# Kernel matmuls directly behind the chunk inputs, late pieces between them, and routing of two token tiles ahead of the third

## What is computed

```python
mod = silu(cond) @ w_ada + b_ada            # 1024 x 6144: shift, scale, gate, twice
h = rms_norm(x) * (1 + sc1) + sh1
u = h @ ssm_w_in
# per 16-channel group, both directions: complex diagonal recurrence of 64 states
h_t = a * h_(t-1) + B u_t;  y = u * D + Re(C h) of both directions
m = gelu(y) @ w_glu;  x = x + g1 * (val * sigmoid(gate))
h2 = rms_norm(x) * (1 + sc2) + sh2
scores = sigmoid(h2 @ router_w); biased = scores + router_b
# best of 4 groups by the sum of its two largest, then the two best experts in it;
# weights = their scores over their sum
y = sum over the chosen e of weight_e * ((silu(h2 @ w_gate[e]) * (h2 @ w_up[e])) @ w_down[e])
x = x + g2 * y;  out = rms_norm(x)
```

## Time and profile before

| | us |
|---|---|
| Median of 3 runs | 860.6 (858.01 to 864.39) |
| The profiled execution | 861.62 |
| Its span in the trace | 859.3 |
| PE busy | 741.9 (86%) |
| DVE busy | 301.7 (35%) |
| ACT busy | 184.9 (22%) |

### The profile page before, as it was taken

How to read it: one execution, slowest core, us unless ns; L and a number is a source line. 1 busy time by engine, 2 the same in 40 slices (tenths; PEclk the granted TensorE clock), 3 DMA queues, 4 the chain that set the end, 5 groups by cost and what they waited for, 6 DMA issues and landing times.

```text
span 859.3 us, 22717 instructions
## 1 busy us (share of the span) xinstructions
PE 741.9 (86%) x9653; PEld 410.0 (48%) x9654; DVE 301.7 (35%) x861; ACT 184.9 (22%) x389; POOL 56.1 (7%) x98
## 2 busy tenths in 40 slices
PE   5799777487989985999997999999999999999830
PEld 5345453176554455545552644554554555455320
DVE  3788769998004235112211111201201212111017
ACT  3554241111022231022211021201201202221113
POOL 1000000530010001100000000000000000000000
PEclk9889897756999985999999999999999999999975
DMA  8900439770108680899999999999999999999933
GB/s 340 412 18 2 167 130 400 281 252 6 51 19 282 208 333 1 314 409 409 411 410 411 409 410 411 409 411 410 410 410 380 412 410 411 410 410 410 411 112 152
DMA packets 70010, 259.15 MB, mean 302 GB/s; under 512 B 10728, under 2 KB 10776, under 8 KB 65864
## 3 DMA queue, kind: packets, MB, share of 16 engines
q1 hardware_dynamic: 66968, 254.02, 75.3%
q0 software_dynamic: 1632, 3.20, 1.0%
q10 hardware_dynamic: 1360, 1.19, 0.6%
HBM read 252.49 MB, written 6.29 MB: 301 GB/s over the span
## 4 chain that ended last, share of the span: by engine, by line
issue 56%; PE 23%; DVE 9%; DMA 3%; POOL 3%; ACT 2%; POOLq 2%; ACTq 1%; SPq 0%; DVEq 0%
PE ps L1035 6%; PE ps L1095 3%; PE ps L984 2%; PE ps L887 2%; PE ps L970 1%; PE ps L927 1%; POOL y_scratch L501 1%; DVE sreg L1336 1%; PE ps L819 1%; PE ps L792 1%; ACTq L665 1%; DVE vreg L1336 1%; POOLq L519 1%; PE ps L992 1%; PE ps L946 1%
## 5 line engine op out<-in xcount | busy, mean ns | idle before, releaser
L1129 PE MATMUL ps<-ring,vreg 128*32 128x512 f32 x2240 | 245.7, 593 | 14.3 <-DMA ring<-in_moe_w_up 9.6
L1129 PEld LDWEIGHTS ps<-ring,vreg 128*32 128x32 f32 x2240 | 72.2, 110 | 180.6 <-issue 160.3
L1136 PE MATMUL ps<-ring,vreg 128*32 128x256 f32 x2240 | 124.2, 380 | 0.0
L1121 PEld LDWEIGHTS ps<-vreg,sreg 128*128 128x128 f32 x816 | 96.1, 196 | 15.1 <-issue 13.4
L1121 PE MATMUL ps<-vreg,sreg 128*128 128x96 f32 x816 | 99.8, 280 | 1.5 <-DVE vreg L1567 1.5
L1597 DVE TENSOR_TENSOR vreg<-vreg,ps 128x256 f32<-128x256 f32 x48 | 17.3, 415 | 223.5 <-ACT vreg L743 223.5
L1136 PEld LDWEIGHTS ps<-ring,vreg 128*32 128x32 f32 x2240 | 71.2, 110 | 46.8
L1608 DVE COPY vreg<-ps 32x256 f32<-32x256 f32 x96 | 40.7, 424 | 105.8 <-PE ps L1136 103.3
L755 ACT ACTIVATE vreg<-ps 32x256 f32<-32x256 f32 x96 | 35.8, 373 | 148.1 <-PE ps L1136 146.1
L743 ACT ACTIVATE vreg<-ps 128x256 f32<-128x256 f32 x48 | 15.0, 384 | 210.0 <-PE ps L1129 210.0
L1035 PE MATMUL ps<-ring 128*128 128x512 f32 x128 | 56.1, 595 | 1.4 <-issue 0.7
(11 more groups left out here) (268 smaller groups left out, 590.2 us busy)
## 6 DMA issues: line engine op xcount, KB each, us to landing
ring<-in_moe_w_gate SPq DMA_DIRECT2D x128, 512.0 KB, 12.9
ring<-in_moe_w_up SPq DMA_DIRECT2D x128, 512.0 KB, 14.4
ring<-in_moe_w_down SPq DMA_DIRECT2D x128, 512.0 KB, 12.7
ring<-in_w_ada SPq DMA_DIRECT2D x24, 1024.0 KB, 11.0
ring<-in_ssm_w_glu SPq DMA_DIRECT2D x8, 1024.0 KB, 11.9
ring<-in_ssm_w_in SPq DMA_DIRECT2D x8, 512.0 KB, 21.8
ring<-y_scratch SPq DMA_DIRECT2D x6, 512.0 KB, 6.3
tmat<-ada_rows SPq DMA_DIRECT2D x4, 512.0 KB, 5.4
```

The source lines that it names most:

```text
L1121: last = pe.matmul(bank[:, col * CAP:(col + 1) * CAP], h2[:, t, k * P:(k + 1) * P], onehot[:, t, :], start=(t == 0), stop=(t == NT - 1))
L1129: last = pe.matmul(ps[t][32 * j:32 * j + 32, :], xgT[:, k, 32 * t:32 * t + 32], w[:, :, 256 * j:256 * j + 256], start=(k == 0), stop=(k == ...
L1136: last = pe.matmul(ps[3 + t // 2][32 * dj:32 * dj + 32, 256 * (t % 2):256 * (t % 2) + 256], aT[:, t, c2, 32 * j:32 * j + 32], ring[:, KT + ...
```

## The change

- The kernel parts begin directly behind the chunk inputs, with pieces 8 to 15 one behind each part; pieces 16 to 23 follow.
- The late pieces use ten slots: 14 to 17 go to slots 8 to 11 behind `pe_p` 32, 18 to 21 to slots 4 to 7 behind pieces 8 to 11, 22 and 23 to slots 8 and 9.
- ScalarE waits for piece 13 before it writes `kwin`. Half of the 16 small transfers into `tmat` go out on SP's queue, behind the last late piece and ahead of all GLU loads.
- Scores, routing, positions, one-hot and first gather are done for two tiles, then for the third. `first_max` fuses comparison and rank into one operation per tile. The slot numbers start at 1, which saves a subtraction. The weights of the choice are computed after the slot numbers, ahead of the first eviction.

```diff
-LATE_SLOTS = (4, 5, 6, 7, 0, 1, 4, 5, 6, 7, 4, 5, 6, 7, 4, 5)
+LATE_SLOTS = (4, 5, 6, 7, 0, 1, 8, 9, 10, 11, 4, 5, 6, 7, 8, 9)
...
+        def store_t(queue, j, q):
+            row = 64 * (q % 2) + 16 * j
+            queue.dma_start(t_of[row:row + 16, 2 * (q // 2):2 * (q // 2) + 2, :, :].rearrange("p i m w -> p i (m w)"),
+                            kwin[32 * q:32 * q + 16, :, j, :, :].rearrange("p i m w -> p i (m w)")
+                            ).then_inc(ld_tmat, 16)
...
+            sp.wait_ge(pe_p, 32)
             for n in range(KT + 6, KT + 10):
-                sp.wait_ge(pe_ada, n - 5)
                 late_piece(n)
-            sp.wait_ge(pe_p, 32)
-            for k in range(4, KT):
-                load_glu(k)
-            for n in range(KT + 10, 3 * KT):
-                sp.wait_ge(pe_ada, n - 3)
+            for n in range(KT + 10, KT + 14):
+                sp.wait_ge(pe_ada, n - 9)
                 late_piece(n)
-            for k in (2, 3, 0, 1):
-                sp.wait_ge(pe_ada, 2 * KT + (5 + k if k > 1 else 7 + k))
+            for n in range(KT + 14, 3 * KT):
+                sp.wait_ge(pe_ada, n - 7)
+                late_piece(n)
+            sp.wait_ge(act_k, 16)
+            for j in range(L):
+                for q in (2, 3):
+                    store_t(sp, j, q)
+            for k, pieces in ((6, 17), (7, 18), (0, 19), (1, 20), (2, 21), (3, 22), (4, 23), (5, 24)):
+                sp.wait_ge(pe_ada, pieces)
                 load_glu(k)
...
+            act.wait_ge(pe_ada, KT + 6)
             for mq in range(2):
                 act.wait_ge(pe_k, 2 * mq + 2)
...
-                for q in range(4):
-                    row = 64 * (q % 2) + 16 * j
-                    act.dma_start(...)
+                for q in range(2):
+                    store_t(act, j, q)
...
+            scores(0, 2)
             store_h2T(2)
-            act.wait_ge(pe_logit, NT)
-            act.activation(route[:, 0], ...)
+            scores(2, NT)
...
-            for n in range(KT, KT + 6):
-                ada_piece(n)
             for x in range(8):
                 kernel_part(x)
-                if x % 2:
-                    ada_piece(KT + 6 + x // 2)
-            for n in range(KT + 10, 3 * KT):
+                ada_piece(KT + x)
+            for n in range(2 * KT, 3 * KT):
                 ada_piece(n)
...
-            gather_x(0, 0, KT)
+            pe.wait_ge(oh_early, 1)
+            for k in range(4):
+                for t in range(2):
+                    gather_first(k, t)
+            pe.wait_ge(dve_mask, 2)
+            pe.matmul(ps[7][:, 2 * NE:3 * NE], tri_less, route[:, 20, 2], start=False, stop=True, skip_group_check=True)
+            pe.matmul(ps[7][:, 3 * NE:4 * NE], tri_ones, route[:, 20, 2], start=False, stop=True, skip_group_check=True
+                      ).then_inc(pe_pos, 1)
+            for k in range(4, KT):
+                for t in range(2):
+                    gather_first(k, t)
+            pe.wait_ge(oh_ready, 1)
+            for k in range(KT):
+                last = gather_first(k, 2)
+            last.then_inc(xt_ps, 1)
...
+            def first_max(val, top, key, rk, t0, t1, out, scale):
+                step(dve.tensor_reduce(top[:, t0:t1], val[:, t0:t1], AX.X, ALU.max))
+                for t in range(t0, t1):
+                    step(stt(key[:, t], val[:, t], top[:, t], rk[:, t], ALU.is_equal, ALU.mult), t == t1 - 1)
+                step(dve.tensor_reduce(top[:, t0:t1], key[:, t0:t1], AX.X, ALU.max))
+                for t in range(t0, t1):
+                    step(ts(out[:, t], key[:, t], top[:, t], scale, ALU.is_equal, ALU.mult), t == t1 - 1)
...
+            route_groups(0, 2)
+            route_experts(0, 2)
+            step(tt(mask[:, 0:2], oh[0][:, 0:2], oh[1][:, 0:2], ALU.add))
+            step(cp(earlier[:, NE:2 * NE], mask[:, 0, :]), False)
+            step(tt(earlier[:, 2 * NE:3 * NE], mask[:, 0, :], mask[:, 1, :], ALU.add), False)
+            step(tt(earlier[:, 3 * NE:4 * NE], mask[:, 0, :], mask[:, 1, :], ALU.add))
+            dve.sem_inc(dve_mask, 1)
+            dve.wait_ge(act_score, 2)
+            route_groups(2, NT)
             dve.wait_ge(pe_pos, 1)
+            step(stt(posm[:, 0:2], place[:, 0:2], 1.0, mask[:, 0:2], ALU.add, ALU.mult))
+            tokens_of(0, 0, 2).then_inc(oh_early, 1)
+            route_experts(2, NT)
+            tt(mask[:, 2], oh[0][:, 2], oh[1][:, 2], ALU.add).then_inc(dve_mask, 1)
+            dve.wait_ge(pe_pos, 2)
+            dve.wait_ge(dve_mask, 2)
+            step(stt(posm[:, 2], place[:, 2], 1.0, mask[:, 2], ALU.add, ALU.mult))
+            tokens_of(0, 2, NT).then_inc(oh_ready, 1)
...
             ins.then_inc(dve_slot, 1)
+            weights_of_choice()
```

More of the change, by code:

```diff
@@ L226, in build @@
         ld_ada = [sem(f"ld_ada{i}") for i in range(len(ADA_SLOTS))]
-        ld_late = [sem(f"ld_late{i}") for i in range(8)]
+        ld_late = [sem(f"ld_late{i}") for i in range(NU)]
         ld_win = [sem(f"ld_win{k}") for k in range(KT)]
@@ L1190, in expert, with gather_first @@
                         last.then_inc(unit_free, 1)
-            gather_x(0, 0, KT)
+            def gather_first(k, t):
+                bank, col = (ps[5], k) if k < 5 else (ps[6], k - 5)
+                return pe.matmul(bank[:, col * CAP:(col + 1) * CAP], h2[:, t, k * P:(k + 1) * P], onehot[:, t, :],
+                                 start=(t == 0 and k in (0, 5)), stop=(t == NT - 1), skip_group_check=True)
+            pe.wait_ge(oh_early, 1)
[13 more added lines that the diff above has]
+            last.then_inc(xt_ps, 1)
             pe.wait_ge(dve_cmax, 1)
@@ L1498, in _ @@
                                      for b in range(4)], dve_h2)
+            step(dve.memset(earlier[:, 0:NE], 0.0), False)
+            oh = [route[:, 10], route[:, 11]]
+            mask = route[:, 20]
+            def first_max(val, top, key, rk, t0, t1, out, scale):
[5 more added lines that the diff above has]
+                    step(ts(out[:, t], key[:, t], top[:, t], scale, ALU.is_equal, ALU.mult), t == t1 - 1)
@@ L1551, in _ @@
-            for k in range(2):
-                step(tt(route[:, 16 + k], sc, oh[k], ALU.mult))
-                step(dve.tensor_reduce(cmb[:, k, :], route[:, 16 + k], AX.X, ALU.add))
-            wsum = route[:, 18, 0, 0:NT]
-            step(tt(wsum, cmb[:, 0, :], cmb[:, 1, :], ALU.add))
-            step(dve.reciprocal(wsum, wsum))
-            for k in range(2):
-                step(tt(cmb[:, k, :], cmb[:, k, :], wsum, ALU.mult))
-            dve.wait_ge(pe_pos, 1)
-            place = ps[7][:, 0:NT * NE].rearrange("p (t e) -> p t e", t=NT)
@@ L1587, in _, with weights_of_choice @@
             ins.then_inc(dve_slot, 1)
+            def weights_of_choice():
+                for k in range(2):
+                    step(tt(route[:, 16 + k], route[:, 0], oh[k], ALU.mult))
+                    step(dve.tensor_reduce(cmb[:, k, :], route[:, 16 + k], AX.X, ALU.add))
+                wsum = route[:, 2, 0, 0:NT]
+                step(tt(wsum, cmb[:, 0, :], cmb[:, 1, :], ALU.add))
+                step(dve.reciprocal(wsum, wsum))
+                for k in range(2):
+                    step(tt(cmb[:, k, :], cmb[:, k, :], wsum, ALU.mult))
+            weights_of_choice()
             def evict_x(nth):
```

103 lines of the change are left out of this document (43 added, 60 removed).

## The result

| | before | after |
|---|---|---|
| Median of 7 runs each, us | 859.92 (857.7 to 864.39) | 852.15 (850.34 to 855.91) |
| Ratio, 95% interval | | 0.9902 [0.9877, 0.9927] |
| Profiled execution, span | 861.62, 859.3 | 851.2, 849.5 |
| Ratio measured once more (e11 below) | | 0.9917 [0.9893, 0.994] |

So 7 to 8 us came instead of the 13.6 forecast (860.6 to 847). The time lies inside the range, but just above both the 851.5 at which the forecast itself ended and the 852.0 for which "faster" was said.

A forecast was written before the change was run, and what follows sets the result against it. The expert loop was taken as load-bound at about 410 GB/s, ending a fixed time after its start, which two earlier chains set. 861.6 less 10.0 (state-space part) less 4.1 (routing) gave 847.5, by the median 847; range 842 to 855.

The forecast's parts named there:

- y_state starts: Context state matmuls: start at 178.9 behind the scan's first half, 12.0 us earlier, at worst 6.0.
- y_state takes: Context state matmuls: 15.5 us instead of 13.9, so 1.6 us lost (0 to 3.6).
- the last piece waits for its data: Late pieces on TensorE: pieces 22 or 23 waiting for data was named as a sign of a wrong forecast.
- rival (c): Kernel parts: code is no limit, the new order avoids the gaps, full 12.0 us come back, 845.5; chance 0.08.
- the last group ends ahead of the third break: Kernel matmuls: with 26 fewer instructions ahead, the last kernel part ends at about 152 instead of 159.2.
- (a): First chain stays late: y_inside at 172, y_state at 184.8 and slow, gain 4.4 instead of 10, 853; chance 0.16.
- (d): GLU and latent y_state: TensorE stays at 1.2 GHz after standing for the scan, slower, up to 873.5; chance 0.02.
- The stores: Convolution tile: eight stores on each of two queues issue in 5.3 us instead of 10.63; last landing 4 us later.
- Routing: Routing and gather before the loop: copies released by VectorE at 338.4 instead of 342.75, gain 4.3, net 4.1 us.
- Rival (b): Routing gains nothing: more operations, weights ahead of the eviction eat the gather's saving; gain 1, 850.6; chance 0.12.
- The clock: Lower TensorE clock costs 0.4 us (0 to 2) in the GLU matmuls and 0.2 at the loop's start.
- whatever moves 344.30 moves the end by as much: Expert loop: it ends a fixed time after the first expert's matmuls at 344.30, as its loads bound it.

The follow-up runs named there:

- e11: The changed kernel measured once more, unaltered, as partner of e12: ratio 0.9917 to the kernel before, median 852.35 us.
- e10: The changed kernel with only the weights of the choice moved behind the first eviction: ratio 0.9909 to the kernel before.
- e1: The kernel before with only the new order of pieces and kernel parts, ten slots and two store queues; old routing: 0.9929, 856.36 us.
- e5: The changed kernel with all 16 stores on ScalarE's queue, SP holding its GLU loads until the stores landed: ratio 0.9907 to before.
- e6: The changed kernel with idle matmuls where TensorE stands in the routing, before the gather and before the loop: ratio 0.9906 to before.
- e7: The changed kernel with pieces 14 to 23 loaded only in 128 of 2048 columns; total not compared, last kernel part ends at 143.4 us.
- e4: The changed kernel with TensorE's old order of pieces and kernel parts, new slots and two store queues kept: ratio 0.9884 to before.
- e8: The changed kernel with idle matmuls in the routing and weights of the choice behind the first eviction: ratio 0.9856 to before.
- e9: The changed kernel with weights of the choice behind the first eviction and three idle matmuls between first gather and loop: ratio 0.9932 to before.
- e12: The same kernel as e8, measured again beside e11: ratio 0.9893 to the kernel before, median 850.66 us.
- e3: The changed kernel with all 16 convolution-tile stores on ScalarE's queue again, GLU loads not held: ratio 1.0003 to before.
- e2: The kernel before with only the new routing and gather, state-space part as before: ratio 0.9968, 858.72 us.

## Why the prediction was right or wrong

| step | predicted | after | e11 | e10 | e1 |
|---|---|---|---|---|---|
| last kernel part ends | 152 | 145.7 | 148.2 | 153.0 | 152.0 |
| y_inside starts | 165 | 160.0 | 162.8 | 166.4 | 167.6 |
| y_state starts | 178.9 | 175.7 | 176.8 | 178.9 | 179.8 |
| y_state takes | 15.5 | 14.8 | 16.1 | 17.2 | 17.0 |
| context GLU, at 13.97 before | 14.4 | 16.9 | 16.5 | 15.5 | 14.0 |
| latent y_state starts | 216 | 215.3 | 216.9 | 219.2 | 217.9 |
| gate and up, more than before | 0.2 | 4.6 | 4.5 | 4.5 | 3.0 |

**The bound was named rightly, the shift too.** y_state was to start behind the scan's first half, 12.0 us earlier. In after, e5, e6, e7, e10 and e11 it is released by VectorE's queue; in after it comes 15.17 - 3.0 = 12.2 us earlier, on the same scan. In e1, e4, e8, e9 and e12 it is y_inside that ends last, and y_state starts 1.2 to 2.8 us later than the scan would let it; in four of these the last piece waits for its data (0.36 to 1.91 us), which the prediction had named as a sign of being wrong. That the kernel parts are held up beside full DMA, and not by what the new order avoids, e7 and e4 bear out: gaps stay with the new order (1.28 and 3.20 in after; 3.09, 0.87 and 3.48 in e1) and shrink with the loads. So rival (c) falls. The step that the last group ends ahead of the third break came true by the count above. That code is what arrives late stays a reading, since the rows only say issue, but the even spacing speaks for it. The Trainium skill, "Runtime: NRT & Kernel Launch", Instruction fetch mechanics, calls the crossing from block to block mostly hidden; if the gaps are code, that does not hold here beside full queues.

**Rivals (a) and (d).** At 852.15 the time lies nearer to the 853 of (a) than to 847, and that is chance: in the runs with the new front, e3 apart, y_inside starts at 156.1 to 168.2, not at 172, and y_state at 175.7 to 180.7, not at 184.8. The range held because it was wide enough to take in (a), not because the sum was right. Of (d) the beginning is there, GLU matmuls that start at the lower clock, but from 221 on they are at their old 7.13 us for 16.

**The stores: right outcome, wrong reason.** I counted 5.3 us less issue for two queues; it is 3.7 (6.96 against 10.63). e5 shows that one queue does as well, and e3 that the GLU loads beside the stores cost everything. The sentence on SP's order, that the loads stand behind the stores, was in the working, but as something that costs nothing, not as what the change lives on.

**y_state: 1.6 us lost were forecast, 0.9 to 3.3 came.** A gap of 3.6 to 4.1 us in it (1.36 in after), with the eight GLU loads still running. I had named it as a sign of a wrong forecast, and had the loads' cover right (the GLU matmuls never wait for them), but not what they do to the matmuls ahead. e7, where they are over, has no gap and 13.88 us.

**Routing: 4.3 forecast to the first expert, 4.1 measured** (24.25 - 20.14; e2 3.8). The releaser was wrong, the gather and not VectorE's weights, and the number came out because the two lie half a microsecond apart. The early block ran at 3.73 us for 16 instructions and the rest at 5.67, at granted 0.50 and 0.65; I took 4.9 for the rest. Rival (b) falls, but with the slow first gate and up only 2.5 us are left at the second expert (51.73 - 49.23).

**The clock is the mis-sized term.** I priced it at 0.4 us for the GLU matmuls and 0.2 at the loop's start; it is 2.9 and 4.6 by the page's rows of the same matmuls. In the loop 1.7 us lie in the first gate and up and 2.8 in the fifth expert's (1.93 for 8 matmuls and 16.72 for 136, against 1.06 and 14.80), a place I had not looked at: it stands for weights in both kernels, but the clock drops there only in the one after. Three executions of the after's loop (after, e10, e11) give 250.2 to 250.3, so it is no chance of one run; but e5 and e4, whose routing and loop are those of after, have 246.0 and 248.3, and e1, whose routing and loop are those of before, 248.7. What decides it isn't settled: in e5 and e6 the loop starts at 2.4 GHz and keeps it through the fifth expert (14.80), in e12 it starts so too and doesn't (17.53). Nor is it settled how much of it is the change's: the kernel before was profiled once, and e2, which has the same state-space part, takes 16.39 us for the GLU matmuls. The premise "whatever moves 344.30 moves the end by as much" failed: it holds only while TensorE releases the units in time, as before and in e6 (512.9 us from the first weight issue to the end). With the lower clock it is 514.8 to 516.1 in after, e10, e11 and e12; e5 has 514.3 without a pause behind the fifth expert, which stays unexplained.

By e11, whose scan is 1.9 us earlier than before: y_state 14.05 earlier, latent y_state 9.2, first expert 12.6, end 9.1; less 1.9, 7.2 us, as the medians have it (859.17 - 852.35 = 6.8).

## What to carry to other kernels

A small, urgent burst of transfers was decided here less by how fast it is issued than by what bulk runs beside it on another queue: put the bulk behind it, on its queue or with a wait. Where the instructions behind a stand come earlier than before, price the matmuls there, and at stands much later, at both clocks; compare the busy time of unchanged groups first when a gain is missing, and look at it in a second profile of the kernel before, too, before the change is blamed. In a loop bound by its loads, look at what releases their buffers: a pause in the loads is what slow matmuls cost. Two limits half a microsecond apart must be moved together.

## What was not expected of the hardware

The DMA engines can count as full and move little: in 162 to 166 us of e4_old_order, with the stores of the tile inside SBUF under way, the window reads

```profile
162.00:166.00 4.00, 1.04 (x12) 0.12 (x4) 4.00 (x21) 2.37 (x3) 4.00 (x1) 0.89 1.13 146
```

a share of 1.13 at 146 GB/s, where the weight loads of the loop move 411 at 1.02.

GpSimd's two copies of 64 columns behind the last kernel part take as long as VectorE's scan of both streams lasts, not as long as their work: 30.35 us from 145.85 in after, 19.82 from 159.35 before, ending 0.4 to 0.5 us behind the scan's first half in both (176.20 and 179.17). The Trainium skill, "SBUF — State Buffer", Who interferes with whom, has a VectorE operation with two inputs in SBUF and a GpSimd operation that reads SBUF exclude each other at a shared port; the traces agree, though no run took the scan away. Nobody waited for these copies.

The same instructions up to there ended the scan's first half at 175.7 us in after, 176.8 in e11 and 178.9 in e10, 3 us apart. In after TensorE ran at the higher clock early in the program (four transposes at 39.55 took 0.66 us, 1.12 at 40.76 in e11 and 40.84 in e10), but e11 and e10 are alike in that, so it doesn't explain the difference between those two; that is left open.
